# Down pieces between the taps, held-back pieces and earlier splits in a hybrid decoder layer on Trainium2

## Chip, cores and metric

The kernel runs on one core of one Trainium2 chip. The metric is the device time of one execution in microseconds (us), lower is better. Everything is one launch: one decoder layer for a prompt of 1024 tokens and 8 decode sequences of 4 tokens, 1056 columns in all.

## What is computed

The reference, cut to what matters here (`branches` stands for four token mixers, which the change doesn't touch):

```python
def trunk_layer(x, pe, ...):
    h = rmsnorm(x, lp['norm_mix'])
    z = h @ lp['w_in']
    branches = jnp.stack([o_a, o_b, o_c, o_d], axis=2)
    proj = jnp.einsum('blnc,ncd->blnd', branches, lp['w_branch'])
    gates = jax.nn.sigmoid(gl.reshape(B, L, N_BRANCH, D_MODEL))
    x = x + jnp.sum(gates * proj, axis=2) @ lp['w_out']
    u = rmsnorm(x, lp['norm_ffn']) @ lp['w_up']
    u, ffn_new = causal_dwconv(ffn_hist, u, lp['conv_f_w'], lp['conv_f_b'])
    ua, ub = jnp.split(u, 2, axis=-1)
    x = x + (jax.nn.gelu(ua) * ub) @ lp['w_down']
    x = x + jax.nn.sigmoid(rmsnorm(x, lp['norm_ple']) @ lp['w_ple_gate']) * (pe @ lp['w_ple'])
```

D_MODEL is 1024, D_FF 2816, all data float32.

## The kernel before

Activations lie transposed, 128 channels on the partitions and 1056 tokens along them. Each product of float32 numbers is made of three on TensorE: every operand is split into a rounded high part and a low part (the rest), and high by high, high by low and low by high are added up in PSUM. So `Uh`/`Ul` are the two parts of a weight tile (128 x 1024, from the raw tile `uraw`, two buffers), `Dh`/`Dl` those of a round's down weights (from `draw`), `Gh`/`Gl` those of the gated feed-forward rows, `mwh`/`mwl` those of the branch weights (from `mwb`), `Hh`/`Ml` those of the mixed rows. ScalarE makes nearly all high parts, GpSimd the low parts of weights, VectorE the low parts of rows. A matmul takes 128 channels by 352 tokens, three of them span the 1056.

The order of the work on each engine is written out by hand, with a semaphore for each hand-over; an engine runs its instructions in that order, so a wait holds up all behind it.

**Gate stage** (`m_round`, four rounds of eight gates u = 0 to 7). In each round TensorE makes five gate products (u = 3 to 7; `Uh[:, v % 2]`) of 72 matmuls and eight branch products of 18; ScalarE takes the sigmoid, VectorE multiplies and sums up (`m_added`). Three gates come back from memory (`early_gate`, SyncE). The branch weights come in two halves q per round: SyncE loads `mwb` (`branch_weights`), ScalarE makes `mwh[:, q]` (`branch_high`), GpSimd `mwl[:, q]` (`branch_low`). For the next round's q = 0, `branch_high` stands at the end of ScalarE's round, behind the sigmoid of u = 7. SyncE loads the second half (`branch_weights(i, 1)`) once the first is split, and behind it on its queue the second early gate.

**Output blocks.** Eight weight tiles of w_out follow. Before the first, ScalarE makes `Uh[:, 0]` (`tile_high(0, 0)`) and then the high parts of the eight mixed rows; VectorE makes their low parts (`mixed_low`), four of them ahead of the last gate's product and sum.

**Feed-forward** (`u_round`, rounds i = 0 to 10, two chunks q of 128 channels each, each with two halves: the GeLU side and the other). Per chunk TensorE runs two up products of 72 matmuls (11.65 us each at the pace of the trace) into the two 3-bank slabs of PSUM. VectorE scales the result by the norm (`u_free`), ScalarE adds the first tap and the bias (`u_tap`), VectorE adds the other two taps, each with small operations for the decode sequences. ScalarE applies GeLU, VectorE multiplies the halves (`split_raw`), ScalarE makes `Gh[:, q]`, VectorE `Gl[:, q]` (`g_ready`).

The down product of round i - 1 (`down`) stands behind the two up products of chunk 0 of round i: 24 pieces (8 output blocks by 3 spans of tokens), 6 matmuls each, the first three on `Gh`/`Gl` chunk 0 and the others on chunk 1. Piece n goes to bank `DOWN_BANKS[n % 8]`, and from n = 8 on must wait until VectorE has added piece n - 8 to `X` (`d_added`). VectorE adds all 24 after the taps of that chunk:

```python
if q == 0 and not isinstance(i, int):
    for n in range(PIECES):
        dve.wait_ge(S("d_done"), i * PIECES + (n + 1 - PIECES))
        add_down(n)
```

After round 10 stands `down(10)`: TensorE makes the first half (chunk 0) of pieces 0 to 7 while the last gate is still being made, waits for it (`g_ready`), makes their second halves, and goes on with pieces 8 to 23. Behind each output block ScalarE and VectorE prepare the last norm (`spread`, `low`, `square_sum`), on which the embedding gate's product waits.

Of the kernel before, what the change touches and what calls it, by code (L numbers as in the profile page):

```python
# [70 lines left out]
MIX_POOL = 4  # L71
TURN_OF = (1, 2, 0, 3, 0, 1, 2, 3)
# [34 lines left out]

DOWN_BANKS = (0, 1, 2, 6, 7, 3, 4, 5)
# [109 lines left out]
def program(nc, a, o):  # L218
    with ExitStack() as ctx:
# [209 lines left out]
        def _(sp):  # L429
# [214 lines left out]
            sp.wait_ge(S("d_lo"), NF // 2)  # L644
            sp.dma_start(draw, a["wpl"]).then_inc(S("d_in"), 16)
            sp.wait_ge(S("g_ready"), NF)
# [11 lines left out]
        def _(pe):  # L658
# [455 lines left out]
            def down(i):  # L1114

                pe.wait_ge(S("d_lo"), i + 1)
                last = isinstance(i, int) and i == 10
                freed = 22 if last else (i * 2 + 3)

                def start(n):  # L1120
                    b = DOWN_BANKS[n % 8]
                    if n >= 8:
                        pe.wait_ge(S("d_added"), i * PIECES + (n - 7))
                    elif n == 0:
                        pe.wait_ge(S("u_free0"), freed)
                    elif b == 3:
                        pe.wait_ge(S("u_free1"), freed)

                def half(n, k):
                    d, (t0, m) = n // 3, SPANS[n % 3]  # L1130
                    b = DOWN_BANKS[n % 8]
                    if n == 0:
                        pe.wait_ge(S("g_ready"), i * 2 + (k + 1))
                    for w, x in ((Dh, Gh), (Dh, Gl), (Dl, Gh)):
                        ins = nc.tensor.matmul(psb(b), w[:, k, d], x[:, k, t0:t0 + m],  # L1135
                                               start=(k == 0 and w is Dh and x is Gh), stop=(k == 1 and w is Dl))
                    if k == 1:
                        ins.then_inc(S("d_done"), 1)
                ahead = 8 if last else 0
                for n in range(ahead):  # L1140
                    start(n)
                    half(n, 0)
                for n in range(ahead):
                    half(n, 1)
                for n in range(ahead, PIECES):
                    start(n)
                    half(n, 0)
                    half(n, 1)

            def u_round(i):  # L1150
                first = isinstance(i, int) and i == 0
                for q in range(2):
                    for half in range(2):
                        pe.wait_ge(S("w_lo"), i * 4 + (ULO + 2 * UP + 2 * q + half + 1))
                        if first and q == 0:
                            if half == 0:
                                pe.wait_ge(S("r_added"), KD)
                            else:
                                pe.wait_ge(S("n1_ln"), 4)
                        elif q == 0:  # L1160
                            pe.wait_ge(S(f"u_free{half}"), i * 2)
                        elif first:
                            pe.wait_ge(S(f"u_free{1 - half}"), 1)
                        else:
                            last = max(n for n in range(PIECES) if DOWN_BANKS[n % 8] // 3 == half)
                            pe.wait_ge(S("d_added"), i * PIECES + (last + 1 - PIECES))
                        first_block = first and q == half == 0
                        dense3(1 - half if first and q == 0 else half, (Uh[:, half], Ul[:, half]), normed_x, KD,
# [1201 lines left out]
```

## Time and profile before

| | |
|---|---|
| median of 3 runs | 1963.89 us (1963.49 to 1965.94) |
| profiled execution | 1966.18 us, span 1964.5 us |
| TensorE (PE) busy | 1873.4 us, 95% |
| TensorE weight loads (PEld) | 1802.0 us, 92% |
| VectorE (DVE) busy | 1007.7 us, 51% |
| ScalarE (ACT) busy | 569.5 us, 29% |
| GpSimd (POOL) busy | 417.1 us, 21% |
| chain that ended last | PE 75%, issue 12%, DVE 6%, ACT 3%, POOL 2% |
| memory traffic | 134.21 MB, 68 GB/s over the span |
| mean granted TensorE clock | 0.985 |

The profile is of one execution on the chip. Times in the rows are us from the span's start, durations of groups too; a row's line is that of the program. A row of the timeline may merge equal neighbours (x3: three in a row, the length is that of all). The bracket behind a row is the time for which the engine stood idle just before, and the instruction that released it. Matmuls overlap, so one that takes 0.32 starts every 0.16. A tile is named by the buffer it lies in: `BIG` holds `X`, `MIX`, the raw weight tiles and other things, `H` the feed-forward rows and `draw`, `ps` and `pst` are PSUM, `masks` holds `mwb`.

### The profile page before, as it was taken

How to read it: one execution, taken by the hardware profiler on the slowest of the kernel's cores; microseconds unless marked ns; L12 is line 12 of the kernel's file. 1: busy time of each engine (PE TensorE's matmuls, PEld its weight loads, DVE VectorE, ACT ScalarE, POOL GpSimd, SP SyncE). 2: the span in 40 equal slices, each digit the busy share in tenths (PEclk: the TensorE clock that was granted, in tenths of full speed). 3: DMA queues.
4: the chain of work that ended last, by engine and by line, in shares of the span. 5: the costliest groups of instructions: out<-in, count | busy, mean ns of one | idle time of the engine just before them, and what ended most of it. 6: DMA issues, size and time to landing. Idle time of an engine off the chain costs nothing.

```text
span 1964.5 us, 28684 instructions
## 1 busy us (share of the span) xinstructions
PE 1873.4 (95%) x11857; PEld 1802.0 (92%) x11857; DVE 1007.7 (51%) x1170; ACT 569.5 (29%) x764; POOL 417.1 (21%) x211
## 2 busy tenths in 40 slices
PE   8999998799899999999999999999999999998998
PEld 5899888797678999999999999999999999998998
DVE  6922473643575122221434765766766766575532
ACT  4223423215464122121333322221221231132620
POOL 1323212112112032121221211221121121021221
PEclk9999999899999999999999999999999999999999
DMA  5212112114414131212311110110111111011121
GB/s 193 36 65 75 60 60 69 60 50 175 120 52 160 41 109 63 89 67 99 109 66 65 65 44 21 64 43 21 64 53 38 37 59 43 26 64 44 41 77 44
DMA packets 54290, 134.21 MB, mean 68 GB/s; under 512 B 12834, under 2 KB 28738, under 8 KB 51906
## 3 DMA queue, kind: packets, MB, share of 16 engines
q1 hardware_dynamic: 42114, 105.40, 15.5%
q0 software_dynamic: 5184, 19.01, 3.0%
q10 hardware_dynamic: 6912, 8.65, 1.2%
q8 instruction: 60, 0.98, 0.2%
q14 instruction: 20, 0.16, 0.0%
HBM read 110.82 MB, written 22.31 MB: 68 GB/s over the span
## 4 chain that ended last, share of the span: by engine, by line
PE 75%; issue 12%; DVE 6%; ACT 3%; POOL 2%; DMA 1%; SPq 1%; ACTq 0%; POOLq 0%; DVEq 0%
PE ps L701 49%; PE ps L683 7%; PE ps L1135 7%; PE pst L1135 2%; PE ps L846 2%; PE ps L664 2%; POOL Ul L2154 1%; DVE H L2060 1%; PE ps L767 1%; PE ps L925 1%; DVE H L2049 1%; PE pst L946 1%; ACT H L1589 1%; PE ps L959 1%; PE ps L670 1%
## 5 line engine op out<-in xcount | busy, mean ns | idle before, releaser
L2178 POOL TENSOR_TENSOR Ul<-BIG,Uh 128x1024 fp32r<-128x1024 f32 x60 | 145.1, 2419 | 735.6 <-ACT Uh L1533 681.7
L701 PE MATMUL ps<-Nh,Uh 128*128 128x352 f32 x1248 | 271.0, 325 | 3.8 <-issue 2.1
L701 PE MATMUL ps<-Fl,Uh 128*128 128x352 f32 x1248 | 269.5, 324 | 0.0
L701 PE MATMUL ps<-Nh,Ul 128*128 128x352 f32 x1248 | 269.4, 323 | 0.0
L701 PEld LDWEIGHTS ps<-Nh,Uh 128*128 128x128 f32 x1248 | 212.9, 189 | 5.0 <-issue 4.8
L701 PEld LDWEIGHTS ps<-Nh,Ul 128*128 128x128 f32 x1248 | 214.9, 188 | 0.0
L701 PE MATMUL ps<-Hh,Uh 128*128 128x352 f32 x936 | 204.4, 327 | 9.5 <-DVE Ml L1971 4.2
L701 PEld LDWEIGHTS ps<-Fl,Uh 128*128 128x128 f32 x1248 | 212.5, 188 | 0.0
L701 PE MATMUL ps<-Hh,Ul 128*128 128x352 f32 x936 | 202.5, 324 | 0.0
L701 PEld LDWEIGHTS ps<-Hh,Uh 128*128 128x128 f32 x936 | 160.2, 190 | 11.9 <-issue 6.1
L701 PEld LDWEIGHTS ps<-Hh,Ul 128*128 128x128 f32 x936 | 161.4, 189 | 0.0
L701 PE MATMUL ps<-Hl,Uh 128*128 128x352 f32 x744 | 160.6, 324 | 0.0
L1994 DVE TENSOR_TENSOR BIG<-BIG,ps 128x1056 f32<-128x1056 f32 x32 | 40.1, 1254 | 232.2 <-PE ps L701 222.9
L2057 DVE SCALAR_TENSOR_TENSOR H<-H,small 128x1023 f32<-128x1023 f32 x88 | 113.0, 1284 | 70.3 <-ACT H L1589 68.8
L1135 PE MATMUL ps<-Gh,Dh 128*128 128x352 f32 x396 | 129.4, 327 | 16.6 <-DVE BIG L2033 10.8
L1135 PE MATMUL ps<-Gl,Dh 128*128 128x352 f32 x396 | 128.1, 323 | 0.0
L1135 PE MATMUL ps<-Gh,Dl 128*128 128x352 f32 x396 | 128.0, 323 | 0.0
L701 PEld LDWEIGHTS ps<-Hl,Uh 128*128 128x128 f32 x744 | 126.7, 188 | 0.0
L683 PE MATMUL ps<-Hh,Uh 128*128 128x352 f32 x376 | 126.5, 336 | 0.0
L683 PE MATMUL ps<-Hh,Ul 128*128 128x352 f32 x376 | 122.0, 324 | 0.0
L683 PE MATMUL ps<-Hl,Uh 128*128 128x352 f32 x376 | 121.8, 324 | 0.0
L2130 POOL CAST Uh<-BIG 128x1024 fp32r<-128x1024 f32 x30 | 34.6, 1154 | 397.3 <-PE ps L683 242.2
(312 smaller groups left out, 3205.1 us busy)
## 6 DMA issues: line engine op xcount, KB each, us to landing
BIG<-in_wu SPq DMA_DIRECT2D x44, 512.0 KB, 3.6
H<-in_wd SPq DMA_DIRECT2D x11, 1024.0 KB, 4.8
BIG<-in_wgl SPq DMA_DIRECT2D x20, 512.0 KB, 4.3
BIG<-in_x SPq DMA_DIRECT2D x16, 528.0 KB, 6.4
gates<-BIG ACTq DMA_DIRECT2D x48, 176.0 KB, 1.9
BIG<-in_wz POOLq DMA_DIRECT2D x16, 512.0 KB, 3.6
BIG<-gates SPq DMA_DIRECT2D x12, 528.0 KB, 4.1
BIG<-in_wge POOLq DMA_DIRECT2D x12, 512.0 KB, 3.6
```

Of the source, the lines that this page charges most:

```text
L664: ins = nc.tensor.matmul(psb(3 * out + g), w[:, k], rhs[:, k, t0:t0 + n], start=first and k == 0, stop=last and k == kk - 1)
L670: ins = nc.tensor.matmul(psb(3 * out + g), w, rhs[:, t0:t0 + n], start=first, stop=last)
L683: ins = nc.tensor.matmul(psb(fill_bank(p)), w[:, u % 2, k], x[:, k, part * PART:part * PART + PART], start=(k == 0 and w is Uh and x is Hh ...
L701: ins = nc.tensor.matmul(psb(3 * out + g), w[wp][:, k], x[xp][k][:, t0:t0 + n], start=(k == 0 and wp == xp), stop=(k == kk - 1 and wp == 1))
L767: ins = nc.tensor.matmul(psb(3 * s + g), w[:, s, k], x[:, k, t0:t0 + n], start=(k == 0 and w is Uh and x is Hh), stop=(k == KD - 1 and w i ...
L846: ins = nc.tensor.matmul(ps[hh][:, cg * 512 + j * P:cg * 512 + j * P + P], kf[:, c * P:c * P + P], qf[:, c * P:c * P + P], start=(j == 0), ...
L925: nc.tensor.matmul(ps[hh][:, at + c0:at + c0 + m], Z[rows, QA + hp, i * P:i * P + P], Z[rows, KA + hp, c0:c0 + m], start=True, stop=c0 + m ...
L1135: ins = nc.tensor.matmul(psb(b), w[:, k, d], x[:, k, t0:t0 + m], start=(k == 0 and w is Dh and x is Gh), stop=(k == 1 and w is Dl))
L1994: v.tensor_tensor(spans(ACC if n == 0 else sig), spans(sig), slab(m_slot(i, u)), ALU.mult)\
L2057: return v.scalar_tensor_tensor(y[:, back:SEQ], x[:, 0:SEQ - back], w, y[:, back:SEQ], ALU.mult, ALU.add)
L2130: nc.gpsimd.tensor_copy(Uh[:, s_], uraw[:, s_]).then_inc(S("w_hi"), 1)
L2178: nc.gpsimd.tensor_tensor(Ul[:, half], uraw[:, half], Uh[:, half].bitcast(F32), ALU.subtract)\
```

## The change

1. VectorE adds two down pieces of round i - 1 right after it has scaled the second half of chunk 0, two more between its two taps, and the rest after the taps.
2. TensorE's `down(9)` covers pieces 0 to 15 only. Pieces 16 to 23 are made after the last up product, in two passes over the chunks; the last gate's chunk 0 is multiplied into `dSQ` and split only when the first pass is over (`g_free`), its low part by GpSimd; the last down weights are split in two parts, output blocks 0 to 4 and 5 to 7. VectorE adds pieces 16 to 20 between the last gate's product and its low part, 21 to 23 behind that.
3. `branch_high(i + 1, 0)` stands behind the gate u = 5 instead of u = 7.
4. The first output block's `Uh[:, 0]` is made by VectorE.
5. The three loads of mixed rows count on semaphores of their own.

The diff, cut to its core:

```diff
@@ SyncE @@
-                    .then_inc(S("mix_in"), 16)
+                    .then_inc(S(MIX_SEMS[n]), 16)
...
@@ TensorE @@
+            for half in range(2):
+                up(10, 0, half)
+            down(9, range(FIRST_N))
+            for half in range(2):
+                up(10, 1, half)
+            for n in range(FIRST_N, PIECES):
+                pe.wait_ge(S("d_added"), 9 * PIECES + (n - 7))
+                if n == FIRST_N:
+                    pe.wait_ge(S("u_free0"), 22)
+                elif DOWN_BANKS[n % 8] == 3:
+                    pe.wait_ge(S("u_free1"), 22)
+                ins = half_piece(n, 0)
+            ins.then_inc(S("g_free"), 1)
+            for n in range(FIRST_N, PIECES):
+                half_piece(n, 1)
+            pe.wait_ge(S("d_lo"), 12)
+            for n in range(8):
+                pe.wait_ge(S("d_added"), 10 * PIECES + (n - 7))
+                half_piece(n, 0)
+            pe.wait_ge(S("g_ready"), NF - 1)
+            for n in range(8):
+                half_piece(n, 1)
...
@@ ScalarE, gate stage @@
+                    if u == 5 and not last:
+                        branch_high(i + 1, 0)
                 if not last:
-                    branch_high(i + 1, 0)
                     for v in range(2):
                         late_high(i + 1, v)
...
-            tile_high(0, 0)
...
@@ ScalarE, last feed-forward round @@
+                            if last:
+                                act.wait_ge(S("d_done"), 9 * PIECES + FIRST_N)
+                                nc.scalar.activation(Dh[:, :, 0:FIRST_D], draw[:, :, 0:FIRST_D], ACT.Copy)\
+                                    .then_inc(S("d_hi"), 1)
...
+                    for half in (range(2) if last and q else range(0) if last else (q,)):
+                        act.wait_ge(S("split_raw"), i * 2 + (half + 1))
+                        if last and half:
+                            act.wait_ge(S("d_done"), 10 * PIECES)
+                        elif last:
+                            act.wait_ge(S("g_free"), 1)
+                        nc.scalar.activation(Gh[:, half], dSQ if last and not half else V[:, 0], ACT.Copy)\
+                            .then_inc(S("split_hi"), 1)
...
@@ VectorE @@
                     if last and u == 7:
+                        dve.wait_ge(S("uw_in0"), 16 * (4 * LATES[0] + 2))
+                        dve.wait_ge(S("m_gate"), 4 * LATE)
+                        v.tensor_copy(Uh[:, 0], uraw[:, 0]).then_inc(S("first_hi"), 1)
                         for k in range(MIX_POOL):
                             mixed_low(k)
...
+                    if first or q and not last:
+                        at, end = 0, 0
+                    else:
+                        at, end = FIRST_N * q, FIRST_N if last and not q else PIECES
...
+                        if half and not q:
+                            add_some(2)
                         dve.wait_ge(S("u_tap"), i * 4 + (2 * q + half + 1))
...
+                        if half and not q:
+                            add_some(2)
                         link(tap(w0, 2),
...
+                    if not q:
+                        add_some(PIECES)
                     dve.wait_ge(S("u_gelu"), i * 2 + (q + 1))
-                    v.tensor_tensor(V[:, 0], V[:, 0], V[:, 1], ALU.mult).then_inc(S("split_raw"), 1)
+                    v.tensor_tensor(dSQ if last and not q else V[:, 0], V[:, 0], V[:, 1], ALU.mult)\
+                        .then_inc(S("split_raw"), 1)
+                    if not last or q:
+                        add_some(5)
+                        dve.wait_ge(S("split_hi"), i * 2 + (q + 1))
+                        v.tensor_tensor(Gl[:, q], V[:, 0], Gh[:, q].bitcast(F32), ALU.subtract)\
+                            .then_inc(S("g_ready"), 1)
+                        add_some(PIECES)
...
@@ GpSimd, last round @@
+                    pool.wait_ge(S("split_hi"), NF - 1)
+                    nc.gpsimd.tensor_tensor(Gl[:, 0], dSQ, Gh[:, 0].bitcast(F32), ALU.subtract).then_inc(S("d_lo"), 1)
```

How the instructions stand now. On VectorE, in a feed-forward round at the second half of chunk 0 (L2049 scales, L2057 to L2065 are the taps, L2033 adds a piece), before:

```order
L2049 TENSOR_TENSOR H<-ps,H 128x1056 [waits dve_chain,u_read1,u_done1]
L2051 REGISTER_ALU
L2057 SCALAR_TENSOR_TENSOR H<-H,small 128x1023 [waits u_tap]
L2060 SCALAR_TENSOR_TENSOR H<-H,small 128x8x3
L2061 SCALAR_TENSOR_TENSOR H<-small,H 128x8
L191 REGISTER_ALU
L2057 SCALAR_TENSOR_TENSOR H<-H,small 128x1022 [waits dve_chain]
L2064 SCALAR_TENSOR_TENSOR H<-H,small 128x8x2
L2065 SCALAR_TENSOR_TENSOR H<-small,H 128x8x2
L191 REGISTER_ALU
L2070 REGISTER_ALU [waits dve_chain]
L2033 TENSOR_TENSOR BIG<-BIG,ps 128x352 [waits d_done]
```

And after the change (L2102 scales, L2112 to L2122 are the taps, L2074 adds a piece):

```order
L2102 TENSOR_TENSOR H<-ps,H 128x1056 [waits dve_chain,u_read1,u_done1]
L2092 REGISTER_ALU
L2074 TENSOR_TENSOR BIG<-BIG,ps 128x352 [waits d_done]
L2092 REGISTER_ALU
L2074 TENSOR_TENSOR BIG<-BIG,ps 128x352 [waits d_done]
L2106 REGISTER_ALU
L2112 SCALAR_TENSOR_TENSOR H<-H,small 128x1023 [waits u_tap]
L2115 SCALAR_TENSOR_TENSOR H<-H,small 128x8x3
L2116 SCALAR_TENSOR_TENSOR H<-small,H 128x8
L193 REGISTER_ALU
L2092 REGISTER_ALU [waits dve_chain]
L2074 TENSOR_TENSOR BIG<-BIG,ps 128x352 [waits d_done]
```

Four adds now stand ahead of the second tap, two of them ahead of the first.

On ScalarE, in the second half of a gate round (L1515 is the sigmoid, L1486 the high part of a gate's weights, L1492 that of the branch weights), before:

```order
L1486 ACTIVATE Uh<-BIG 128x1024 [waits uw_in1]
L1515 ACTIVATE BIG<-ps 128x1056 [waits m_added,m_gate]
L1486 ACTIVATE Uh<-BIG 128x1024 [waits uw_in0]
L1515 ACTIVATE BIG<-ps 128x1056 [waits m_added,m_gate] x2
L1492 ACTIVATE mwh<-masks 128x1024 [waits m_proj,mw_in]
L1486 ACTIVATE Uh<-BIG 128x1024 [waits uw_in0]
L1486 ACTIVATE Uh<-BIG 128x1024 [waits uw_in1]
L1515 ACTIVATE BIG<-BIG 128x1056 [waits early_in0]
L1515 ACTIVATE BIG<-BIG 128x1056 [waits early_in1]
```

After the change (L1540, L1511 and L1517 in the same roles):

```order
L1540 ACTIVATE BIG<-ps 128x1056 [waits m_added,m_gate]
L1511 ACTIVATE Uh<-BIG 128x1024 [waits uw_in1]
L1540 ACTIVATE BIG<-ps 128x1056 [waits m_added,m_gate]
L1511 ACTIVATE Uh<-BIG 128x1024 [waits uw_in0]
L1517 ACTIVATE mwh<-masks 128x1024 [waits m_proj,mw_in]
L1540 ACTIVATE BIG<-ps 128x1056 [waits m_added,m_gate] x2
L1511 ACTIVATE Uh<-BIG 128x1024 [waits uw_in0]
L1511 ACTIVATE Uh<-BIG 128x1024 [waits uw_in1]
L1540 ACTIVATE BIG<-BIG 128x1056 [waits early_in0]
```

The branch weights' row has moved ahead of the last two sigmoids.

On VectorE, behind the last gate's second tap (L2073 multiplies the halves, L2075 makes the low part, L2033 adds pieces of the last down product), before:

```order
L2057 SCALAR_TENSOR_TENSOR H<-H,small 128x1022 [waits dve_chain]
L2064 SCALAR_TENSOR_TENSOR H<-H,small 128x8x2
L2065 SCALAR_TENSOR_TENSOR H<-small,H 128x8x2
L191 REGISTER_ALU
L2072 REGISTER_ALU [waits dve_chain]
L2073 TENSOR_TENSOR H<-H 128x1056 [waits u_gelu]
L2075 TENSOR_TENSOR Gl<-H,Gh 128x1056 [waits split_hi]
L198 REGISTER_ALU
L198 COMPARE_AND_BRANCH
L2033 TENSOR_TENSOR BIG<-BIG,ps 128x352 [waits d_done,u_read1]
L2033 TENSOR_TENSOR BIG<-BIG,ps 128x352 [waits d_done] x2
L2033 TENSOR_TENSOR BIG<-BIG,pst 128x352 [waits d_done] x2
```

After the change (L2128 multiplies, L2133 makes the low part, L2074 adds a piece, the first eight of them held back from the product before):

```order
L2112 SCALAR_TENSOR_TENSOR H<-H,small 128x1022 [waits dve_chain]
L2121 SCALAR_TENSOR_TENSOR H<-H,small 128x8x2
L2122 SCALAR_TENSOR_TENSOR H<-small,H 128x8x2
L2128 TENSOR_TENSOR H<-H 128x1056 [waits u_gelu,dve_chain]
L2074 TENSOR_TENSOR BIG<-BIG,ps 128x352 [waits d_done] x3
L2074 TENSOR_TENSOR BIG<-BIG,pst 128x352 [waits d_done] x2
L2133 TENSOR_TENSOR Gl<-H,Gh 128x1056 [waits split_hi]
L2074 TENSOR_TENSOR BIG<-BIG,ps 128x352 [waits d_done] x3
L2074 TENSOR_TENSOR BIG<-BIG,ps 128x352 [waits d_done,u_read1]
L2074 TENSOR_TENSOR BIG<-BIG,ps 128x352 [waits d_done] x2
```

Five adds now stand between the product and the low part, three behind it.

## Rows read from the trace of the kernel before

**Rows 1.** Waits of TensorE, whole span: total us, times, longest us.
```profile
PE ps L1135 <- DVE BIG L2033: 10.8, 10, 1.1
...
PE ps L1135 <- DVE Gl L2075: 5.8, 1, 5.8
PE ps L701 <- POOL mwl L2162: 4.9, 3, 1.6
```

**Rows 2.** Timeline of TensorE, one down product: start, length (us), line, [idle before it].
```profile
1186.34 0.32 PE L1135 MATMUL ps<-Gh,Dh 128*128 128x352 f32 x1
...
1193.83 0.32 PE L1135 MATMUL ps<-Gh,Dl 128*128 128x352 f32 x1
1195.24 0.43 PE L1135 MATMUL ps<-Gh,Dh 128*128 128x352 f32 x1 [1.08 <-DVE BIG L2033]
```

**Rows 3.** Timeline of VectorE in that round, and one row of ScalarE.
```profile
1186.54 1.26 DVE L2049 TENSOR_TENSOR H<-ps,H 128x1056 f32<-128x1056 f32 x1 [1.39 <-PE ps L701]
1189.14 1.29 DVE L2057 SCALAR_TENSOR_TENSOR H<-H,small 128x1023 f32<-128x1023 f32 x1 [1.34 <-ACT H L1589]
1190.34 2.44 DVE L2060 SCALAR_TENSOR_TENSOR H<-H,small 128x24 f32<-128x24 f32 x1
...
1194.66 1.38 DVE L2033 TENSOR_TENSOR BIG<-BIG,ps 128x352 f32<-128x352 f32 x3
...
1222.51 1.26 DVE L2049 TENSOR_TENSOR H<-ps,H 128x1056 f32<-128x1056 f32 x1 [7.55 <-PE ps L701]
...
1187.83 1.27 ACT L1589 ACTIVATE H<-H,small 128x1056 f32<-128x1056 f32 x1 [6.95 <-DVE H L2049]
```

**Rows 4.** Timelines of TensorE, GpSimd and ScalarE at a gate round's start.
```profile
692.26 0.75 PE L701 MATMUL ps<-Ml,mwh 128*128 128x352 f32 x3 [1.62 <-POOL mwl L2162]
...
689.84 2.37 POOL L2162 TENSOR_TENSOR mwl<-masks,mwh 128x1024 fp32r<-128x1024 f32 x1 [26.74 <-ACT mwh L1492]
...
698.05 1.09 ACT L1515 ACTIVATE BIG<-BIG 128x1056 f32<-128x1056 f32 x1 [5.43 <-DMA BIG<-gates]
```

**Rows 5.** Timelines of TensorE, ScalarE, GpSimd and VectorE at the first output block.
```profile
943.85 0.96 PE L701 MATMUL ps<-Hh,Uh 128*128 128x352 f32 x3 [2.83 <-DVE Ml L1971]
...
954.21 0.75 PE L701 MATMUL ps<-Hh,Uh 128*128 128x352 f32 x3 [1.34 <-DVE Ml L1971]
...
939.10 1.05 ACT L1533 ACTIVATE Uh<-BIG 128x1024 fp32r<-128x1024 f32 x1
...
940.22 2.37 POOL L2178 TENSOR_TENSOR Ul<-BIG,Uh 128x1024 fp32r<-128x1024 f32 x1 [26.74 <-ACT Uh L1533]
...
941.22 8.26 DVE L1971 TENSOR_TENSOR Ml<-BIG,Hh 128x1056 fp32r<-128x1056 f32 x4 [12.07 <-ACT Hh L1544]
...
963.74 0.70 DVE L2025 COPY BIG<-BIG 128x1056 f32<-128x1056 f32 x1
```

**Rows 6.** Timelines of TensorE, GpSimd and VectorE at the last gate.
```profile
1801.56 0.32 PE L1135 MATMUL ps<-Gh,Dh 128*128 128x352 f32 x1
...
1811.39 0.66 PE L1135 MATMUL ps<-Gh,Dh 128*128 128x352 f32 x1 [5.82 <-DVE Gl L2075]
...
1795.12 5.31 POOL L2196 TENSOR_TENSOR Dl<-H,Dh 128x2048 fp32r<-128x2048 f32 x1 [34.78 <-ACT Dh L1603]
...
1795.89 4.57 DVE L2064 SCALAR_TENSOR_TENSOR H<-H,small 128x16 f32<-128x16 f32 x1
...
1805.97 1.28 DVE L2057 SCALAR_TENSOR_TENSOR H<-H,small 128x1022 f32<-128x1022 f32 x1
...
1807.67 1.26 DVE L2073 TENSOR_TENSOR H<-H 128x1056 f32<-128x1056 f32 x1
...
1814.44 0.52 DVE L2033 TENSOR_TENSOR BIG<-BIG,ps 128x352 f32<-128x352 f32 x1 [0.36 <-PE ps L1135]
```

**Rows 7.** Timeline of TensorE where the last down product is over.
```profile
1834.35 0.73 PE L701 MATMUL ps<-Nh,Uh 128*128 128x352 f32 x3 [2.10 <-issue]
```

**Rows 8.** Busy us by engine (PE, PEld, DVE, ACT, POOL) in a stretch, then granted clock.
```profile
1811.00:1816.00 5.00, 4.61 (x20) 4.61 (x21) 2.85 (x6) 3.36 (x4) 2.39 (x1) 0.65 0.60 216
```

More of the change, by code:

```diff
@@ L1111, in last_square, with half_piece, down @@
                 whole(0, cc("mean"), nSQ7, first=False).then_inc(S("norm_sum"), 1)
-            def down(i):
+            def half_piece(n, kk):
+                d, (t0, m) = n // 3, SPANS[n % 3]
+                for w, x in ((Dh, Gh), (Dh, Gl), (Dl, Gh)):
+                    ins = nc.tensor.matmul(psb(DOWN_BANKS[n % 8]), w[:, kk, d], x[:, kk, t0:t0 + m],
+                                           start=(kk == 0 and w is Dh and x is Gh), stop=(kk == 1 and w is Dl))
+                if kk:
+                    ins.then_inc(S("d_done"), 1)
+                return ins
+            def down(i, pieces):
                 pe.wait_ge(S("d_lo"), i + 1)
[L1117 to L1121, printed above, removed]
+                pe.wait_ge(S("g_ready"), i * 2 + 2)
+                for n in pieces:
                     if n >= 8:
@@ L1124, in start @@
                     elif n == 0:
[L1125 to L1148, printed above, removed]
+                        pe.wait_ge(S("u_free0"), i * 2 + 3)
+                    elif DOWN_BANKS[n] == 3:
+                        pe.wait_ge(S("u_free1"), i * 2 + 3)
@@ new lines, in down, with up @@
+                    half_piece(n, 0)
+                    half_piece(n, 1)
+            def up(i, q, half):
+                first = isinstance(i, int) and i == 0
+                pe.wait_ge(S("w_lo"), i * 4 + (ULO + 2 * UP + 2 * q + half + 1))
+                if first and q == 0:
+                    if half == 0:
+                        pe.wait_ge(S("r_added"), KD)
+                    else:
+                        pe.wait_ge(S("n1_ln"), 4)
+                elif q == 0:
+                    pe.wait_ge(S(f"u_free{half}"), i * 2)
+                elif first:
+                    pe.wait_ge(S(f"u_free{1 - half}"), 1)
+                else:
+                    done = PIECES if not isinstance(i, int) else FIRST_N
+                    last = max(n for n in range(done) if DOWN_BANKS[n % 8] // 3 == half)
+                    pe.wait_ge(S("d_added"), i * PIECES + (last + 1 - PIECES))
+                    if isinstance(i, int):
+                        pe.wait_ge(S(f"u_free{half}"), i * 2 + 1)
+                first_block = first and q == half == 0
+                dense3(1 - half if first and q == 0 else half, (Uh[:, half], Ul[:, half]), normed_x, KD,
+                       ("n2_h", 0) if first_block else None, (5, last_square) if first_block else None)\
+                    .then_inc(S(f"u_done{half}"), 1)
@@ L1150, in u_round @@
             def u_round(i):
-                first = isinstance(i, int) and i == 0
                 for q in range(2):
                     for half in range(2):
[L1154 to L1168, printed above, removed]
-                               ("n2_h", 0) if first_block else None, (5, last_square) if first_block else None)\
-                            .then_inc(S(f"u_done{half}"), 1)
-                    if q == 0 and not first:
-                        down(i - 1)
@@ L1173, in _ @@
-            rounds(pe, 11, u_round)
-            down(10)
+                        up(i, q, half)
+                    if q == 0 and not isinstance(i, int):
+                        down(i - 1, range(PIECES))
+            rounds(pe, 10, u_round)
+            for half in range(2):
[10 more added lines that the diff above has]
+                ins = half_piece(n, 0)
@@ L1582, in u_round @@
                             if q or not isinstance(i, int) or i:
[L1583 removed]
+                                act.wait_ge(S("split_raw" if last and q else "g_ready"), i * 2 + q)
                             fp = small[:, 64:72]
```

72 lines of the change are left out of this document (47 added, 25 removed).

## Prediction

> **What bounds the kernel now.** I read the page first: TensorE is busy 95% of the span, so a gain is a wait taken off TensorE, and nothing else. The view of waits on TensorE then names those that this change aims at [rows 1]: 10 waits for a down piece to be added (10.8 us, the longest 1.1), one of 5.8 us for the last gate's low part, three for the low part of the branch weights (4.9 us); two more, before the first output block, stand in [rows 5]. The timeline around one of each says who is late. In each of these rows the bracket at the end is TensorE's idle time.
>
> **Part 1, down pieces between the taps (rounds 1 to 10).** TensorE starts a down product at 1186.34 and has issued 48 matmuls by 1193.83, 0.159 us apart [rows 2], so one piece (6 matmuls) takes 0.957 us and the 8 PSUM banks last 7.66 us. Piece 8 needs piece 0 added. VectorE is then still at the second half: scaling at 1186.54, taps from 1189.14, a 24-column part of them held to 2.44 us, and the first add only at 1194.66 [rows 3]. TensorE starts again at 1195.24, 1.25 us after it could have, and its first matmul takes 0.43 instead of 0.32: 1.36 us lost. The change puts two adds behind the scaling. VectorE ends that at 1187.80 and waits for ScalarE's first tap (1187.83, 1.27 long) until 1189.14 [rows 3]. Piece 0 is done at about 1187.5 and piece 1 at 1188.45, an add takes 0.46 (three in 1.38), so both end by 1188.9: free, inside a wait of 1.34. The next two stand between the taps and delay them by 0.9; the fifth add then ends near 1196.1. TensorE needs add 1 at 1193.99, add 3 at 1195.9, add 5 at 1197.8: margins of 5, 2 and 1.7 us. All adds still follow their pieces at the end (VectorE 0.46 against TensorE 0.957), and VectorE's product afterwards is followed by 7.55 idle until the next up half ends (1222.51 [rows 3]), so what moves does not come back. Ten rounds by 1.36: **-13.6**. Bounds: 10 by 1.08 if the restart cost stays (-10.8), and -14.
>
> **Part 2, branch weights split behind the sixth gate.** At 689.84 GpSimd begins the low part of the first half of the branch weights, released by ScalarE, which had waited for the eighth gate; TensorE starts the branch product at 692.26 after 1.62 idle [rows 4]. SyncE asks for the weights after the fourth gate already. Moved two gates earlier, the split costs ScalarE about 1.05 (the tile of the same size in [rows 5]) and GpSimd 2.4 while both wait for a gate. Per round 1.62 plus the restart seen in part 1 (1.36 - 1.08 = 0.28), so 1.9; three rounds: **-5.7**. What is late next? ScalarE's second early gate comes at 698.05 after 5.43 of waiting on its load [rows 4]; that load is queued on SyncE behind the second half's weights, and these behind this very split, so it comes earlier too. The sigmoid and product of that gate then end before TensorE needs the slot. If they did not, the part would keep about a third (-2).
>
> **Part 3, first output block on VectorE.** TensorE waits 2.83 for the first mixed row and 1.34 for the sixth [rows 5]. ScalarE splits the weight tile first (939.10, 1.05), then GpSimd (940.22, 2.37) holds VectorE's first subtraction, recorded from 941.22. VectorE, idle there, now copies the tile: a copy of 1056 columns took 0.70 [rows 5], begun as the gate ends at 938.2. GpSimd then starts near 938.95 and ends near 941.3, not 942.6, and the first row is ready 1.25 earlier. The second wait hangs on the same chain of VectorE (four rows, product, sum, sixth row), which has its own waits for GpSimd, so the saving of both together is that 1.25: **-1.3**. The clock could change it: the matmuls after the 2.83 gap run at half pace (0.96 for three). If the half clock only moves behind the second wait, which gets longer, the part is +0.4; if it goes and the second wait shrinks too, -3.
>
> **Part 4, the last hand-over.** Let 0 be 1801.56, where the last up product ends. Before: 24 half-piece matmuls, 5.82 idle, and the second halves from 9.83 [rows 6]; the first matmuls then run at the 1.2 GHz level (mean granted clock 0.65 over those 5 us [rows 8]), and the third add ends at 1814.96, or 13.4. From there VectorE and ScalarE work through the tail without a break (TensorE, finished, waits 2.10 for them [rows 7]), so what counts is when that third add ends. Now 8 pieces of the product before (7.66 us) are held back, the end of the up product comes 7.66 earlier, and the pieces fill the gap in two passes, 0 to 7.7. Then a chain of single buffers decides. ScalarE copies the first gate half when the first pass ends (4.2 to 5.3), GpSimd subtracts its low part (2.37 for 1024 columns, so 2.45). VectorE is at its second tap from 4.41 to 5.69 (1805.97, 1.28). The row that matters is 1795.89: a VectorE operation on 16 columns lasting 4.57 beside GpSimd's at 1795.12, 5.31 [rows 6]. So I let the small operations behind the tap wait until GpSimd is done, at 8.1, and the product at 1807.67 (6.1) starts at 8.6 and ends at 9.8. The first held-back add ends at 10.3, and only then may the last product's first piece start: 2.4 idle. Five adds (2.2), the gate's low part (1.25) and one add more set the sixth piece at 13.8; the first halves end at 15.4 at full pace, 15.8 at the lower clock; I take 15.6. Three pieces and their adds take 2.3 at full pace: 17.9. Against 13.4 + 7.66 = 21.1 that is **-3.2**. Bounds: nothing gained (0), and the whole 5.82 plus the slow start, -7.5.
>
> The Trainium skill, SBUF — State Buffer (Reading the diagram), says that a GpSimd operation and a VectorE operation with two SBUF inputs lock the shared port pair against each other for the whole instruction. By that rule the hold at 8.1 is certain and an add, with one input in PSUM, is not held. Without such a lock the product would end at 7.4, the first halves at 12.8, and this part would be -6.0. The row at 1795.89 agrees with the rule.
>
> Semaphore names and the split of the last down weights (5 and 3 columns of blocks) cost nothing: GpSimd's three shorter operations lie behind the adds of the last product, 8 us ahead of the piece that needs the second.
>
> **The sum.** 13.6 + 5.7 + 1.3 + 3.2 = 23.8. The profiled execution took 1966.18 (span 1964.5), so it would take 1942.4. It lies 2.3 above the median of the three runs, 1963.89, and the forecast is for that median: **1940.1**.
>
> **Rivals.**
> 1. *The stall moves to piece 12.* The adds between the taps push the later ones back, and if the fifth ends over 1.7 us later than I work out, TensorE waits there instead of at piece 8. With half of each wait back: 1940.1 + 6.8 = 1947. For it: two adds in front of two taps. Against: the margin [rows 2, 3]. 5%.
> 2. *The gate stage keeps its wait.* The early gate's load or the sum held by GpSimd ends last instead of the split. Part 2 gives 2, the others stay: 1943.8. 10%, inside the main range.
> 3. *The last hand-over gives nothing or costs.* The held-back pieces, the half-clock restart and the second buffer wait eat the cover; part 4 at 0 to +2: 1943.3 to 1945.3. 12%.
> 4. *Slower.* GpSimd's subtraction of the down weights (5.31 at 1795.12 [rows 6], 4.6 of it work) falls into the second half's taps, where the adds now wait behind it. The fifth add would end 4.6 later, at 1200.7 instead of 1197.8: 2.9 idle, 3.2 lost where 1.36 was. Ten rounds give +18 and the rest -10.2: 1972. It decides above 2.4 us of new wait per round. Against: ScalarE releases that subtraction only in the round's other half. 3%.
> 5. *The change does nothing of what it says*, since another wait ends at the same place everywhere: 1963. Against: at 1194.66 TensorE had its weights and operands and waited for one add. 2%.
>
> **How the numbers follow.** The forecast as worked out, with small misses, has 68%. The range holds it and rivals 1 to 3: up from 1940.1 by the unlucky ends of parts 2 and 4 together (3.7 + 3.2) to 1947, down by the lock not biting (2.8) and part 3's far end (1.7) and a little of part 1 to 1935. A measurement of this kernel can tell about 0.2% (3.9 us) from no change. Faster by more than that holds all but rivals 4 and 5 and some unseen mishap: 0.94; within 0.2%: 0.03; slower: 0.03.
>
> **What would show it.** TensorE's waits for an add fall from ten to one or two, each in the last hand-over, and each round is 1.36 us shorter. The three waits for the low branch weights are gone, and the second early gate no longer waits 5 us. The wait for the first mixed row is near 1.6. In the last hand-over TensorE waits about 2.4 for an add, then about 1 for another, and a 16-column VectorE operation shows about 2.5. I am wrong if a wait for an add stands at piece 12 in each round, if the branch product still waits for its weights, or if the final tail from the third add on is longer than before.

## The result and the profile after

The changed kernel took 1940.69 us (median of 4 runs, 1938.64 to 1941.88) where the one before took 1963.69 (4 runs): ratio 0.9883, 95% interval 0.9866 to 0.99. The forecast was 1940.1, in 1935 to 1947. Its profiled execution took 1940.31. From the page of the changed kernel, the span, two engines (us, share, instructions) and the chain that ended last:

```profile
span 1938.6 us, 28620 instructions
...
PE 1866.9 (96%) x11857; PEld 1798.5 (93%) x11857; DVE 1001.2 (52%) x1170; ACT 568.4 (29%) x764; POOL 422.1 (22%) x213
...
PE 89%; DVE 4%; issue 3%; ACT 2%; SPq 1%; DMA 1%; POOL 0%; ACTq 0%; POOLq 0%; DVEq 0%
```

TensorE's share of the chain went from 75% to 89%. The waits of TensorE that answer to [rows 1] (in total, times, longest):

```profile
PE ps L703 <- DVE Ml L2009: 4.3, 3, 1.7
...
PE ps L1120 <- DVE BIG L2074: 2.2, 1, 2.2
```

Ten waits for an add have become one, in the last hand-over. The three for the low part of the branch weights are gone; for a low part of the mixed rows (`Ml`) there are three, in the first output block, where there were two. The chain of work that ended last, in order of time, shows two rounds of the feed-forward stage, 69.56 us apart (start, length, what):

```profile
1384.78 2.87 PE ps L1120 x18
...
1454.34 2.87 PE ps L1120 x18
```

The first operations of the down product are in the chain as TensorE's own work: it waits for nobody there. VectorE in one round of the changed kernel, which answers to [rows 3]:

```profile
1176.11 1.26 DVE L2102 TENSOR_TENSOR H<-ps,H 128x1056 f32<-128x1056 f32 x1 [1.72 <-PE ps L703]
1177.29 0.51 DVE L2074 TENSOR_TENSOR BIG<-BIG,ps 128x352 f32<-128x352 f32 x1
1178.03 0.52 DVE L2074 TENSOR_TENSOR BIG<-BIG,ps 128x352 f32<-128x352 f32 x1 [0.23 <-PE ps L1120]
1178.71 1.29 DVE L2112 SCALAR_TENSOR_TENSOR H<-H,small 128x1023 f32<-128x1023 f32 x1 [0.16 <-ACT H L1614]
1179.92 2.44 DVE L2115 SCALAR_TENSOR_TENSOR H<-H,small 128x24 f32<-128x24 f32 x1
...
1182.62 0.52 DVE L2074 TENSOR_TENSOR BIG<-BIG,ps 128x352 f32<-128x352 f32 x1
1183.06 0.51 DVE L2074 TENSOR_TENSOR BIG<-BIG,pst 128x352 f32<-128x352 f32 x1
...
1185.19 0.52 DVE L2074 TENSOR_TENSOR BIG<-BIG,pst 128x352 f32<-128x352 f32 x1
```

The two first adds fit between the scaling and the first tap, whose own wait for ScalarE falls to 0.16. Two more stand at 1182.62, and the fifth begins at 1185.19, ends at 1185.71 and was wanted 11.5 us after the product's start at 1175.91, at 1187.4: the margin of 1.7 that the prediction gave. At the start of a gate round, answering to [rows 4] (GpSimd, ScalarE):

```profile
687.38 5.80 POOL L2214 TENSOR_TENSOR Ul<-BIG,Uh 128x1024 fp32r<-128x1024 f32 x2 [23.36 <-ACT Uh L1511]
...
688.15 2.05 ACT L1540 ACTIVATE BIG<-BIG 128x1056 f32<-128x1056 f32 x2
...
697.62 1.09 ACT L1540 ACTIVATE BIG<-BIG 128x1056 f32<-128x1056 f32 x1 [6.47 <-DMA BIG<-gates]
```

GpSimd now starts the round with the gates' weights, ScalarE takes two sigmoids without a wait between them, and the wait for a load has moved to the third (6.47), where nobody needs it yet.

A table of stages is the surest comparison here. Its marks are starts in the timelines of one profiled execution of each kernel: the sigmoid of the eighth gate in the first and in the last round (687.76 and 938.15 in the kernel before), the first matmul of the first down product, the first matmul behind the last up product (1801.56 [rows 6]) and that of the embedding gate (1834.35 [rows 7]). The kernels other than the first two are those of the experiments below.

| kernel, us | to the first eighth gate | three gate rounds | to the first down product | feed-forward | to the embedding gate | rest |
|---|---|---|---|---|---|---|
| before | 687.8 | 250.39 | 177.21 | 686.20 | 32.79 | 130.1 |
| after | 685.3 | 244.72 | 176.32 | 664.69 | 37.08 | 130.5 |
| adds_alone | 681.0 | 250.31 | 177.17 | 672.35 | 32.79 | 129.6 |
| branch_alone | 686.3 | 244.72 | 177.22 | 685.91 | 32.89 | 129.7 |
| copy_alone | 687.3 | 250.35 | 176.37 | 685.94 | 32.88 | 129.6 |
| hold_alone | 686.0 | 250.36 | 177.20 | 678.33 | 37.08 | 130.1 |
| first_pair | 683.5 | 244.72 | 176.37 | 664.69 | 37.10 | 130.1 |
| beside_lock | 685.9 | 244.72 | 176.37 | 664.69 | 35.79 | 129.6 |
| rows_vector | 684.6 | 244.72 | 175.62 | 664.69 | 37.09 | 130.2 |
| both | 685.1 | 244.72 | 175.64 | 664.69 | 35.79 | 131.3 |
| tail_order | 685.8 | 244.72 | 176.36 | 664.69 | 34.09 | 130.5 |
| rows_late | 686.4 | 244.72 | 174.46 | 664.69 | 36.39 | 129.6 |
| best | 687.4 | 244.72 | 174.46 | 664.70 | 34.09 | 129.7 |

The four middle columns repeat to within 0.1 where nothing was changed in them (feed-forward within 0.3), with one exception: rows_late has 36.39 in the last hand-over, where it runs the same instructions as the kernels with 37.08 to 37.10. That is TensorE's clock, as shown below. The first column, in which the kernels differ in nothing but the place of one split on ScalarE, varies by 6.8 and the last by 1.7. Both go with the clock: in the last column the first 15 to 16 us ran at a mean granted clock of 1.00 in adds_alone (129.6), 0.89 in the kernel before (130.1) and 0.80 in both (131.3); over the first column it was 0.98 in adds_alone (681.0) and 0.97 in the kernel before (687.8). So the medians differ by 2 or 3 us for reasons that lie outside of every edit, and the edits are read from the stages. Before to after they give 5.67 + 0.89 + (686.20 + 32.79 - 664.69 - 37.08 = 17.22) = 23.8; the spans differ by 25.9, because the first column gave another 2.5 and the last took back 0.4.

### The profile page after: what moved, and what is told of

Its sections match the earlier page's. It is cut to its first block, busy times and chain, and to the rows that moved or that the text cites. A ratio compares the mean times of both kernels' runs of the same rounds, so it can differ in the third digit from the quotient of the medians.

```text
span 1938.6 us, 28620 instructions
## 1 busy us (share of the span) xinstructions
PE 1866.9 (96%) x11857; PEld 1798.5 (93%) x11857; DVE 1001.2 (52%) x1170; ACT 568.4 (29%) x764; POOL 422.1 (22%) x213
## 3 DMA queue, kind: packets, MB, share of 16 engines
q1 hardware_dynamic: 42114, 105.40, 15.8%
## 4 chain that ended last, share of the span: by engine, by line
PE 89%; DVE 4%; issue 3%; ACT 2%; SPq 1%; DMA 1%; POOL 0%; ACTq 0%; POOLq 0%; DVEq 0%
PE ps L703 59%; PE ps L1120 10%; PE ps L685 7%; PE pst L1120 3%; PE ps L848 2%; PE ps L666 2%; PE ps L769 1%; PE ps L927 1%; PE pst L948 1%; PE ps L961 1%; PE ps L672 1%; DVE Ml L2009 0%; DVE BIG L1868 0%; SPq L521 0%; DMA masks<-in_wb 0%
## 5 line engine op out<-in xcount | busy, mean ns | idle before, releaser
L2112 DVE SCALAR_TENSOR_TENSOR H<-H,small 128x1023 f32<-128x1023 f32 x88 | 115.5, 1313 | 58.2 <-ACT H L1614 57.0
```

The costliest lines, as they stand in the source:

```text
L2112: return v.scalar_tensor_tensor(y[:, back:SEQ], x[:, 0:SEQ - back], w, y[:, back:SEQ], ALU.mult, ALU.add)
```

## Experiments

**Each part alone.** Four kernels timed together, each against the kernel before.

The first, on the kernel before, lets VectorE take two adds ahead of the second half's first tap and two behind it:

```diff
+                        if half and not q:
+                            add_some(2)
                         dve.wait_ge(S("u_tap"), ...)
...
+                        if half and not q:
+                            add_some(2)
                         link(tap(w0, 2), ...)
```

> The kernel before with the four adds between the taps only. My theory: the wait for an add at piece 8 is gone in all ten rounds and nothing takes its place, -13.6 us (-13.0 to -14.2), rounds 69.6 apart. Rival (the gains of the parts are not separate: the adds pay only because the gate stage or the last hand-over changed too): clearly less than 12, with new waits for d_added in the rows.

Ratio 0.992 (0.9903 to 0.9937), median 1948.4. The feed-forward stage fell from 686.20 to 672.35 (-13.85; -13.56 against the two kernels with 685.9), and none of the other three middle columns moved. The part needs none of the others.

The second moves ScalarE's high part of the branch weights behind the sixth gate, on the kernel before:

```diff
+                    if u == 5 and not last:
+                        branch_high(i + 1, 0)
                 if not last:
-                    branch_high(i + 1, 0)
```

> The kernel before with the branch weights split behind the sixth gate only. My theory: three waits of 1.62 with their restarts go, -5.6 us (-5 to -6); no wait for the low branch weights left. Rival (the early gate's load ends last instead): -2, with TensorE waiting for a freed slot at the third gate of a round.

Ratio 0.9973 (0.9958 to 0.9989). The three gate rounds fell by 5.67, 1.89 each, and no wait of TensorE for the low branch weights is left. The early gate's load is not what ends last.

The third, on the kernel before with the three semaphores of the loads, gives VectorE the copy ahead of the first output block:

```diff
                     if last and u == 7:
+                        v.tensor_copy(Uh[:, 0], uraw[:, 0]).then_inc(S("first_hi"), 1)
...
-            tile_high(0, 0)
```

> The kernel before with the first output block's high part made by VectorE, and the three loads of mixed rows on semaphores of their own. My theory: the chain of VectorE starts 1.2 earlier and the block ends 1.2 earlier, -1.2 us. Rival (the half clock after the long gap is what the part removes, and the gain is the clock's): -3, or +0.4 where the half clock only comes later.

Ratio 0.9989 (0.9978 to 1.0), which is not told from no change by the runs. The stage is 0.84 shorter; the copy and the semaphores of the loads were not tried apart. Whether VectorE's earlier start or the clock explains the gain shows in branch_alone, a kernel without the copy, at the same place (TensorE's three waits in the first output block, and below them the busy us of the engines from 936.88 to 940.88 with the granted clock behind them):

```profile
936.74 0.72 PE L701 MATMUL ps<-Hh,Uh 128*128 128x352 f32 x3 [2.82 <-DVE Ml L1972]
...
942.44 0.75 PE L701 MATMUL ps<-Hh,Uh 128*128 128x352 f32 x3 [1.10 <-DVE Ml L1972]
...
947.10 0.75 PE L701 MATMUL ps<-Hh,Uh 128*128 128x352 f32 x3 [1.49 <-DVE Ml L1972]
...
936.88:940.88 4.00, 4.00 (x26) 4.00 (x27) 4.00 (x3) 3.91 (x5) 2.90 (x1) 1.00 0.33 122
```

The gap of 2.82 is as long as before the change (2.83 [rows 5]), but here the clock stayed at its upper level, 1.00, and the matmuls run at 0.72 for three. The stage nevertheless takes 177.22, as with the half clock. TensorE merely waits once more (1.10 for the fourth row, then 1.49 for the sixth): VectorE's chain sets the end, and the clock is not what this part gains or loses.

hold_alone is the changed kernel with the other three parts put back as they were, of which the main lines are:

```diff
-                    if u == 5 and not last:
-                        branch_high(i + 1, 0)
                 if not last:
+                    branch_high(i + 1, 0)
...
+            tile_high(0, 0)
...
-                        v.tensor_copy(Uh[:, 0], uraw[:, 0]).then_inc(S("first_hi"), 1)
...
-                        if half and not q:
-                            add_some(2)
```

> The changed kernel without the adds between the taps, the earlier split and VectorE's copy: the held-back pieces of the last but one down product alone. My theory: -3.3 us against the kernel before, and the four kernels of this batch add up to -23.7, so little is left for interaction. Rival (the held-back pieces pay only with the early adds): 0 to -1.

Ratio 0.9983 (0.9972 to 0.9994). Feed-forward and last hand-over together fell from 718.99 to 715.41, by 3.58. The four parts add up to 13.85 + 5.67 + 0.84 + 3.58 = 23.9, against 23.8 in the changed kernel: no interaction of any size. The things that make up the fourth part (the pieces held back, the gate's low part on GpSimd, the down weights split in two) were not taken apart. The waits of hold_alone for an add:

```profile
PE ps L1120 <- DVE BIG L2071: 13.0, 11, 2.2
```

Ten at the rounds' place (10.8 as in [rows 1]) and the one of 2.2 in the last hand-over.

**How many early adds are needed.**

On VectorE in the changed kernel the second pair goes back behind the tap:

```diff
-                        if half and not q:
-                            add_some(2)
                         link(tap(w0, 2), ...)
```

> The changed kernel with only the first pair of adds (ahead of the first tap); the second pair goes behind the taps. My theory: piece 10 needs the third add at about 1195.9 in the times of the kernel before, and behind the taps it would end at about 1195.1, so no wait comes and the time is that of the changed kernel (within 0.5 us): two early adds are enough. Rival (both pairs are needed): a wait for an add at piece 10 in each round, 0.3 to 0.8 us, so +3 to +8.

Feed-forward 664.69, to the hundredth that of the changed kernel; ratio against before 0.9879 (0.9863 to 0.9896). VectorE in a round of it:

```profile
1176.29 0.52 DVE L2074 TENSOR_TENSOR BIG<-BIG,ps 128x352 f32<-128x352 f32 x1 [0.23 <-PE ps L1120]
...
1182.50 0.52 DVE L2074 TENSOR_TENSOR BIG<-BIG,ps 128x352 f32<-128x352 f32 x1
```

The third add ends at 1183.02. TensorE's timeline has the product's first matmul at 1174.18 in this kernel, and piece 10 begins 10 x 0.957 = 9.6 later, at 1183.7. Two adds are enough, with 0.7 to spare. Whether one would do was not tried.

**The stall of the last hand-over.** In the changed kernel (TensorE, VectorE, GpSimd, and the engines' busy us with the clock over 4 us), answering to [rows 6 to 8]:

```profile
1771.04 0.32 PE L1120 MATMUL ps<-Gh,Dh 128*128 128x352 f32 x1
...
1781.11 0.40 PE L1120 MATMUL ps<-Gh,Dh 128*128 128x352 f32 x1 [2.23 <-DVE BIG L2074]
...
1776.66 2.44 DVE L2121 SCALAR_TENSOR_TENSOR H<-H,small 128x16 f32<-128x16 f32 x1
...
1787.32 1.41 DVE L2074 TENSOR_TENSOR BIG<-BIG,ps 128x352 f32<-128x352 f32 x3 [2.17 <-PE ps L1120]
...
1776.32 2.74 POOL L2263 TENSOR_TENSOR Gl<-H,Gh 128x1056 fp32r<-128x1056 f32 x1 [9.37 <-ACT Gh L1642]
...
1781.00:1785.00 4.00, 3.89 (x15) 3.92 (x16) 4.00 (x8) 3.97 (x5) 0.00 (x0) 0.58 0.01 4
```

The first row is the end of the up product, the second TensorE's restart. The 16-column operation at 1776.66 is held 2.44 until GpSimd's low part is done, the product starts late, the held-back adds with it, and TensorE waits 2.23 and then runs near half pace (0.58).

What the half pace costs shows in rows_late (an experiment on the first output block, below), which runs the same instructions here and also waits 2.23, but whose clock stayed at its upper level:

```profile
1783.58 0.43 PE L1120 MATMUL ps<-Gh,Dh 128*128 128x352 f32 x1 [0.58 <-DVE BIG L2077]
...
1780.24:1784.24 4.00, 3.31 (x19) 3.04 (x20) 4.00 (x8) 3.97 (x5) 0.00 (x0) 1.00 0.02 4
```

At full pace TensorE comes to the sixth piece before its bank is free and waits a second time, 0.58. The second halves of the eight pieces still start earlier, 14.85 after the up product where the changed kernel has 15.53, and the stretch to the embedding gate is 36.39 instead of 37.08. So the lower clock costs 0.69 here.

On VectorE in the changed kernel, the held-back adds go between the two operations of the tap:

```diff
-                        link(tap(w0, 2),
+                        main = tap(w0, 2)
+                        if half and q and last:
+                            add_some(5)
+                        link(main,
```

> The changed kernel with the five held-back adds put right behind the last gate's second tap, ahead of the 16-column operations that wait for GpSimd. My theory: an add reads one operand from PSUM and runs while GpSimd holds the port, so these five cost nothing, the first pieces of the last product start at about +8.2 instead of +10.1 after the up product's end, the three remaining adds fit into ScalarE's copy, and the second halves start about 3 us earlier: -3 us against the changed kernel (-2 to -4). Rival (an add is held by GpSimd as the small operations are): the adds end no earlier than now, 0 to +1.

Ratio 0.9885 (0.9864 to 0.9905). The stretch fell by 1.29, not 3:

```profile
1779.77 0.43 PE L1120 MATMUL ps<-Gh,Dh 128*128 128x352 f32 x1 [0.24 <-POOL Gl L2266]
...
1777.30 1.37 DVE L2074 TENSOR_TENSOR BIG<-BIG,ps 128x352 f32<-128x352 f32 x3
1778.59 0.94 DVE L2074 TENSOR_TENSOR BIG<-BIG,pst 128x352 f32<-128x352 f32 x2
1779.46 0.30 DVE L2124 SCALAR_TENSOR_TENSOR H<-H,small 128x16 f32<-128x16 f32 x1
...
1788.59 3.20 DVE L2055 TENSOR_TENSOR Fl<-BIG,Nh 128x1056 fp32r<-128x1056 f32 x1 [1.18 <-ACT Nh L1576]
...
1776.96 2.75 POOL L2266 TENSOR_TENSOR Gl<-H,Gh 128x1056 fp32r<-128x1056 f32 x1 [9.37 <-ACT Gh L1642]
1786.45 1.85 POOL L2268 TENSOR_TENSOR Dl<-H,Dh 128x768 fp32r<-128x768 f32 x1 [6.73 <-ACT Dh L1651]
1788.26 2.42 POOL L2244 TENSOR_TENSOR Ul<-BIG,Uh 128x1024 fp32r<-128x1024 f32 x1
```

The first half of the theory holds. Three adds take 1.37 and two 0.94 while GpSimd is at its 2.75, the 16-column operation behind them takes 0.30, TensorE waits 0.24 instead of 2.23, and no slow matmuls follow. (The clock fell behind the wait of 2.23 in four of the five kernels that have it, and behind the 0.24 in none of the four that have that.) In the rows of its timeline the third add of the last product ends at 14.3 after the up product, not 17.7. But then the tail's first subtraction at 1788.59 takes 3.20: it meets GpSimd's two operations at 1786.45 and 1788.26, which used to lie in front of it. Of 3.4, 2.1 were given back there. Against rows_late, where the clock did not fall, the stretch is only 0.60 shorter: the other 0.69 of the 1.29 is the clock's.

On top of beside_lock GpSimd makes the embedding tile's low part before it waits for the last down product:

```diff
+                    tile_low(PLE, 0)
                     pool.wait_ge(S("d_hi"), 12)
...
-                    tile_low(i + PLE, q)
+                    if q or not isinstance(i, int):
+                        tile_low(i + PLE, q)
```

> The kernel with the adds beside GpSimd's lock, and GpSimd's low part of the first embedding gate's weights ahead of the last down weights' second part. My theory: there the third add ends 3.4 us earlier than in the changed kernel, but only 1.3 reaches the embedding gate, since the tail's first VectorE subtraction was held from 1788.6 until GpSimd's two operations were done (3.20 us instead of 1.26). With the order turned, GpSimd is done about 1.8 us earlier, so the stretch from the last up product to the embedding gate falls from 35.8 to about 34.1. Rival (the tail is bound by ScalarE, which starts its first spread only when it is through with its own splits): 35.8 as before.

The stretch to the embedding gate is 34.09, as expected (1.70 less than in beside_lock); ratio 0.9865 (0.9846 to 0.9884), median 1937.67:

```profile
1784.65 2.41 POOL L2244 TENSOR_TENSOR Ul<-BIG,Uh 128x1024 fp32r<-128x1024 f32 x1 [5.04 <-ACT Uh L1559]
1787.02 1.85 POOL L2269 TENSOR_TENSOR Dl<-H,Dh 128x768 fp32r<-128x768 f32 x1
...
1788.48 1.51 DVE L2055 TENSOR_TENSOR Fl<-BIG,Nh 128x1056 fp32r<-128x1056 f32 x1 [1.18 <-ACT Nh L1576]
```

GpSimd is done at 1788.9 and holds the subtraction for 0.25 only.

**The first output block.** In the changed kernel (TensorE, VectorE, GpSimd), answering to [rows 5]:

```profile
934.57 0.72 PE L703 MATMUL ps<-Hh,Uh 128*128 128x352 f32 x3 [1.66 <-DVE Ml L2009]
...
940.27 0.74 PE L703 MATMUL ps<-Hh,Uh 128*128 128x352 f32 x3 [1.10 <-DVE Ml L2009]
...
944.93 0.75 PE L703 MATMUL ps<-Hh,Uh 128*128 128x352 f32 x3 [1.52 <-DVE Ml L2009]
...
930.12 0.69 DVE L2029 CAST Uh<-BIG 128x1024 fp32r<-128x1024 f32 x1 [9.10 <-PE ps L703]
932.08 8.13 DVE L2009 TENSOR_TENSOR Ml<-BIG,Hh 128x1056 fp32r<-128x1056 f32 x4 [1.26 <-ACT Hh L1569]
...
943.62 3.60 DVE L2009 TENSOR_TENSOR Ml<-BIG,Hh 128x1056 fp32r<-128x1056 f32 x3
...
930.90 2.41 POOL L2241 TENSOR_TENSOR Ul<-BIG,Uh 128x1024 fp32r<-128x1024 f32 x1 [25.54 <-DVE Uh L2029]
936.02 3.07 POOL L2249 TENSOR_TENSOR Ml<-BIG,Hh 128x1056 fp32r<-128x1056 f32 x1 [2.72 <-ACT Hh L1569]
```

In rows_vector VectorE makes the fifth row's low part too, GpSimd does not, and GpSimd's next weight tile waits for a later row:

```diff
-                        pool.wait_ge(S("mix_hi"), MIX_POOL + 1)
-                        nc.gpsimd.tensor_tensor(Ml[:, MIX_POOL], ...)
+                        pool.wait_ge(S("mix_lo"), MIX_POOL + 1)
```

> The changed kernel with all low parts of the mixed rows on VectorE and GpSimd's next weight tile moved behind the fifth of them. My theory: the two waits inside the first output block (1.10 and 1.52) come from VectorE being held for GpSimd's two operations; VectorE does the fifth row itself in 1.2 instead of waiting 2.4, so -1.5 us (-1 to -2.5). Rival (VectorE's own work sets the chain): 0 to +1.

Ratio 0.9882 (0.9865 to 0.99); the stage fell by 0.70, half of what was expected, and 0.27 of that lies outside of the first output block (see part 3 below):

```profile
942.20 0.75 PE L703 MATMUL ps<-Hh,Uh 128*128 128x352 f32 x3 [0.83 <-DVE Ml L2009]
...
946.75 0.74 PE L703 MATMUL ps<-Hh,Uh 128*128 128x352 f32 x3 [1.37 <-DVE Ml L2009]
...
940.89 5.80 DVE L2009 TENSOR_TENSOR Ml<-BIG,Hh 128x1056 fp32r<-128x1056 f32 x3
...
942.23 3.35 POOL L2244 TENSOR_TENSOR Ul<-BIG,Uh 128x1024 fp32r<-128x1024 f32 x1 [9.62 <-DVE Ml L2009]
```

The wait for the fourth row went and that for the sixth fell to 0.83, but the weight tile, now behind the sixth row's low part, was split beside the last two rows (three rows in 5.80), and a wait of 1.37, for the eighth row, came in a new place.

The two edits together, rows_vector with beside_lock's diff, make the kernel both:

> The two edits before together on the changed kernel. My theory: they lie in different stages and add up, -4.5 us against the changed kernel, about 1936. Rival (one of them fails as above): the other's share alone.

Ratio 0.9877 (0.986 to 0.9894). By stages the two add up: 175.64 and 35.79, as in the kernels that have one of them.

The next one, on top of rows_vector, lets GpSimd's tile wait until all the rows are written:

```diff
-                        pool.wait_ge(S("mix_lo"), MIX_POOL + 1)
+                        pool.wait_ge(S("mix_lo"), KD - 1)
```

> The kernel with all mixed rows on VectorE, and GpSimd's next weight tile behind the last row instead of the fifth. My theory: the tile's 3.35 us held the sixth and seventh rows, which made the wait of 1.37; behind the rows it holds nobody and is done as the second block starts, so the first block ends about 1 us earlier than in that kernel (0.5 to 1.3). Rival: the second block now waits for its weights instead, 0.

174.46, another 1.16 less; ratio 0.9888 (0.9871 to 0.9905). Three rows take 3.60 and the second block waits 0.19:

```profile
944.00 0.75 PE L703 MATMUL ps<-Hh,Uh 128*128 128x352 f32 x3 [0.81 <-DVE Ml L2009]
...
948.82 0.75 PE L703 MATMUL ps<-Hh,Uh 128*128 128x352 f32 x3 [0.19 <-POOL Ul L2244]
...
942.69 3.60 DVE L2009 TENSOR_TENSOR Ml<-BIG,Hh 128x1056 fp32r<-128x1056 f32 x3
```

**All together.** The kernel best is both with the edits of tail_order and rows_late:

```diff
-                        pool.wait_ge(S("mix_lo"), MIX_POOL + 1)
+                        pool.wait_ge(S("mix_lo"), KD - 1)
...
+                    tile_low(PLE, 0)
                     pool.wait_ge(S("d_hi"), 12)
```

> Both edits with their two forerunners on the changed kernel. By stages: -3 in the last hand-over, -1.7 in the first output block, -4.7 against the changed kernel, about 1936; the runs differ by some 3 us from one to the next in the stages ahead of the gates, so the stages of the trace decide and not the medians. Rival: one edit fails as above.

Median 1935.98 (4 runs, 1934.98 to 1936.96), ratio 0.9854 (0.9838 to 0.9871): 4.7 below the changed kernel's median, and by the stages (176.32 - 174.46) + (37.08 - 34.09) = 4.85, 0.69 of it the clock's.

## Why the prediction was right

1. **Adds between the taps**: -13.6 forecast, -13.6 to -13.9 measured in the stage. The restart cost goes with the wait, which is why it is over 10.8. What the prediction didn't ask is how many of the four early adds are needed; first_pair shows that the second two buy nothing.
2. **Branch weights**: -5.7 forecast, -5.67 measured, with 1.89 a round from a wait of 1.62. The early gate's load came earlier as argued.
3. **Copy on VectorE**: -1.3 forecast, -0.84 to -0.89 measured. Up to the second block it is 1.16 (20.79 to 19.63 between the sigmoid and the add); some 0.27 goes again before the first down product, in each kernel with the copy except those with rows_vector's edit. It goes in one place, at the first up product. TensorE waits there for VectorE's last add of the output blocks, and that add starts 0.62 after the six matmuls that stand before it (L672, from 1030.96) instead of 0.27 (L670, from 1040.24 in the kernel before). Why the add starts later is open. The forecast of a first wait near 1.6 holds (1.66). The total of the waits did not fall (4.3 for 4.2) while the block became shorter: the half clock went, and its time turned into waiting.
4. **Last hand-over**: -3.2 forecast; -3.37 up to the third add's end (17.7 after the up product for 17.9), -3.58 in the stages of hold_alone. The wait of 2.4 is 2.23, the held operation of about 2.5 is 2.44, and the second halves start at 1786.57, 15.5 after the up product where the prediction has 15.6. That they agree so well is partly luck: the prediction took a value between 15.4 at full pace and 15.8 at the lower clock, and the runs have 14.85 at full pace (rows_late) and 15.53 at the lower clock. The chain up to the first held-back add was a little shorter than worked out: it ends at 9.9, not 10.3. The second, shorter wait, forecast at about 1, did not come in the changed kernel: at the lower clock the sixth piece was not reached before its bank was free. At full pace it came, 0.58 in rows_late.

The forecast's sum is 23.8, the stages' 23.8 and the medians' 23.0. That the last is so near is partly luck: the stretches that no edit touches vary by more than the difference. None of the rivals came true. The one for the gate stage would have left TensorE waiting for what hangs on the early gate's load; ScalarE still waits 6.47 for that load, and TensorE has no wait between 684 and 701.

## What to carry to other kernels

Where TensorE stops at a ring of PSUM banks, the consumer needs only as many early adds as bridge its other work, and they are free in a gap that it already spends waiting. When an operation is held by another engine's, as VectorE's with two inputs in SBUF were beside GpSimd's, put in front of it what isn't held; and after freeing one engine look at once at which operations of the others lay in the old gap, since they will now lie in the way. A gain at one place (3.4 in beside_lock) reached the end, but for 0.4, only after the next collision had been moved as well.

## What the runs showed of the hardware

Adds with one operand in PSUM ran at full pace, 0.46 each, next to a GpSimd operation (1777.30, 1.37 for three), while in the changed kernel an operation on 16 columns with both inputs in SBUF was held 2.44 beside the same one, and a subtraction with both inputs in SBUF took 3.20 instead of 1.26 beside the two that follow (1788.59 in beside_lock). This agrees with the Trainium skill, SBUF — State Buffer (Reading the diagram), by which a VectorE operation with two SBUF inputs and a GpSimd operation lock each other out for their whole length. The adds have one SBUF input only, and that was used here as a place for work.

The granted clock after a gap isn't given by the gap's length alone. After 2.83 us TensorE ran at its 1.2 GHz level in the kernel before, after 2.82 us at the same place of branch_alone at the 2.4 GHz level; After 2.23 us it ran at the lower level from the fourth matmul on in the changed kernel, and at the upper level in rows_late, with the same instructions at that place. A difference of 0.7 us in one stage can so be the clock's and not the edit's; the rows of the granted clock tell which.
